# Two transformer layers in one program: an opening in another order, the step between the layers by token tile, expert flags read ahead

## The reference, cut to what matters

```python
def reference(x, c, ..., c_2, ctx_2, ...):
    x = first_block(x, c, ...)
    return second_block(x, c_2, ctx_2, ...)

def first_block(...):
    mod = (silu(c) @ w_ada + b_ada)[:, None, :]
    sh1, sc1, ga1, sh2, sc2, ga2 = split(mod, 6, axis=-1)
    h = rmsnorm(x, ln1_pre) * (1.0 + sc1) + sh1
    proj = h @ w_in                       # attention, HGRN2 and gates
    ...
    x = x + ga1 * rmsnorm(mix, ln1_post)
    h = rmsnorm(x, ln2_pre) * (1.0 + sc2) + sh2
    y = hierarchical_moe(h, ...)          # 32 experts, 2 of them per token
    x = x + ga2 * rmsnorm(y, ln2_post)

def second_block(...):                    # hybrid_layer, then rms_norm(x, final_norm_g)
    h = rms_norm(x, norm_mix_g) * (1 + sc_mix) + sh_mix
    p_in = h @ w_in + b_in
    hc = rms_norm(ctx, norm_mix_g) * (1 + mod_ctx[d:]) + mod_ctx[:d]
    ...
    x = x + g_mix * (merged @ w_out)
    h2 = rms_norm(x, norm_ffn_g) * (1 + sc_ffn) + sh_ffn
    y = moe_ffn(h2, ...)                  # a shared expert, and 64 experts, 8 of them per token
    x = x + g_ffn * y
```

## Time and profile before

| | us |
|---|---|
| median of 3 runs | 2428.25 (2425.47 to 2430.88) |
| the profiled execution | 2415.87 |
| its span | 2414.1 |
| PE busy / DVE / ACT / POOL | 2010.9 / 923.0 / 552.9 / 401.2 |
| granted TensorE clock, mean | 0.933 of full speed |

### The profile page before, as it was taken

How to read it: one execution, slowest core, us unless ns; L and a number is a source line. 1 busy time by engine, 2 the same in 40 slices (tenths; PEclk the granted TensorE clock), 3 DMA queues, 4 the chain that set the end, 5 groups by cost and what they waited for, 6 DMA issues and landing times.

```text
span 2414.1 us, 33274 instructions
## 1 busy us (share of the span) xinstructions
PE 2010.9 (83%) x13566; PEld 1361.5 (56%) x13567; DVE 923.0 (38%) x2043; ACT 552.9 (23%) x1018; POOL 401.2 (17%) x379
## 2 busy tenths in 40 slices
PE   3899989688781698996776998987999998999875
PEld 2677778454341686784444665754555555555432
DVE  2144552532214225215766122224443444434325
ACT  2132412211112214114665110020111111111111
POOL 0000000222211000001100000001444545444320
PEclk8899999699996797899999999978999999999998
DMA  6654530689993212012110122214899999999967
GB/s 258 243 227 175 210 123 12 237 338 417 417 386 134 79 53 70 18 53 79 48 48 2 61 88 104 97 53 169 350 360 357 400 404 402 365 358 395 382 247 311
DMA packets 97403, 514.79 MB, mean 213 GB/s; under 512 B 25154, under 2 KB 26210, under 8 KB 43100
## 3 DMA queue, kind: packets, MB, share of 16 engines
q1 hardware_dynamic: 62592, 449.60, 47.2%
q0 software_dynamic: 29504, 51.31, 6.0%
q10 hardware_dynamic: 5148, 11.59, 1.4%
HBM read 508.87 MB, written 49.81 MB: 231 GB/s over the span
## 4 chain that ended last, share of the span: by engine, by line
PE 68%; DVE 10%; DMA 10%; ACT 7%; issue 3%; ACTq 1%; POOL 0%; SPq 0%; DVEq 0%; POOLq 0%
PE ps L249 29%; PE ps L1689 16%; PE ps L1756 8%; DMA arena<-in_egu 7%; PE ps L1655 2%; ACT arena L2773 2%; DVE arena L2809 2%; PE ps L402 2%; DMA arena<-in_ada 2%; PE ps L1743 1%; ACT arena L2784 1%; PE ps L2758 1%; DMA arena<-y_rows 1%; PE ps L424 1%; ACT arena L267 1%
## 5 line engine op out<-in xcount | busy, mean ns | idle before, releaser
L1689 PE MATMUL ps<-arena 128*64 128x256 f32 x4096 | 479.4, 388 | 54.0 <-DMA arena<-in_egu 35.9
L1689 PEld LDWEIGHTS ps<-arena 128*64 128x64 f32 x4096 | 301.4, 140 | 256.3 <-DMA arena<-in_egu 66.2
L249 PE MATMUL ps<-arena 128*128 128x256 f32 (+4 forms) x1276 | 323.4, 416 | 2.4 <-DVE arena L491 1.3
L249 PEld LDWEIGHTS ps<-arena 128*128 128x128 f32 (+1 forms) x1276 | 229.0, 203 | 92.7 <-issue 71.2
L1756 PE MATMUL ps<-arena 128*64 128x512 f32 x1024 | 243.4, 604 | 37.0 <-issue 29.1
L1637 POOL DMA_INDIRECT arena<-h_rows,arena x160 | 193.2, 1208 | 312.6 <-DVE arena L1618 162.6
L1643 POOL DMA_INDIRECT y_rows<-arena x160 | 160.2, 1002 | 419.2 <-DVE arena L1787 369.6
L1751 DVE COPY arena<-ps 128x256 f32<-128x256 f32 (+1 forms) x96 | 36.5, 380 | 431.9 <-PE ps L1743 431.9
L1730 ACT ACTIVATE arena<-ps 128x256 f32<-128x256 f32 (+1 forms) x96 | 33.4, 348 | 503.8 <-PE ps L1689 503.8
L300 DVE TENSOR_TENSOR wlb<-arena,whb 128x1024 fp32r<-128x1024 f32 (+1 forms) x46 | 55.7, 1213 | 242.1 <-ACT whb L292 242.1
L1756 PEld LDWEIGHTS ps<-arena 128*64 128x64 f32 x1024 | 67.7, 136 | 134.7 <-issue 131.0
(11 more groups left out here) (392 smaller groups left out, 3062.2 us busy)
## 6 DMA issues: line engine op xcount, KB each, us to landing
arena<-in_egu SPq DMA_DIRECT2D x204, 1024.0 KB, 12.4
arena<-in_ed SPq DMA_DIRECT2D x102, 1024.0 KB, 8.4
arena<-in_ada SPq DMA_DIRECT2D x48, 1024.0 KB, 7.1
arena<-in_win SPq DMA_DIRECT2D x33, 1024.0 KB, 4.9
arena<-y_rows SPq DMA_DIRECT2D x20, 1024.0 KB, 13.9
arena<-in_wout SPq DMA_DIRECT2D x8, 1024.0 KB, 6.8
arena<-in_nabias POOLq DMA_DIRECT2D x16, 512.0 KB, 3.9
h_rows<-arena ACTq DMA_DIRECT2D x8, 512.0 KB, 2.9
```

The costliest lines, as they stand in the source:

```text
L249: z = pe.matmul(o, l, r, start=start and i == 0, stop=stop and i == len(pairs) - 1, skip_group_check=check)
L1689: z = pe.matmul(b[64 * j:64 * j + 64, 256 * s:256 * s + 256], XV[:, c, 64 * h:64 * h + 64], wk(k)[:, j * 256:j * 256 + 256], start=k == 0, ...
```

## The change

**Opening.** The 13 constants, and the attention bias table and two norm rows, are issued by POOL at its start; ACT issues only three loads. `x` comes in four transfers. The squares and the norm of `x` run on ACT before it copies the first `ada` sums. `PAIRS[1]` and `PAIRS[2]` change places, so that shift and scale of features 0 to 511 come first; the modulation runs over features 0 to 3 (of eight groups of 128) and then, behind `ada` pieces 2 and 3, over 4 to 7, its scaling by turns on ACT (even) and DVE (odd). The first weights are split in between. The first `win1` product waits for the first half only.

```diff
+        def act_start(act, w):
+            act_first(act, w)
+            act_cact(act, w)
+            act_floor(act, w)
+            act_norm(act, w, n1, x3, scr3, 4, lambda t: ld.to("x", t))
+            for n in range(2):
+                act_ada(act, w, n)
+            act_norm_split(act, w, n1, G1, MOD1[:, 0:8], HP1, range(4))
+            act_ada(act, w, 2)
+            for q in range(2):
+                act_hi(act, w, w1, 0, q, W1S, 2048, [n1.to("n", "T", 7)])
+            act_ada(act, w, 3)
+            act_norm_split(act, w, n1, G1, MOD1[:, 0:8], HP1, range(4, 8))
...
+        def pe_start(pe, w):
+            first, turns = [6, 7], [0, 1, 2, 3, 4, 5]
+            for n in range(2):
+                pe_ada(pe, w, n, first)
...
+            for n in (2, 3):
+                pe_ada(pe, w, n, first)
```

```diff
+            for t in range(4):
+                w.wait_ge(*ca.to("sum", t))
+                act.activation(scr3[:, t, :], sum1(t), ACT.Square, accum_out=small[:, t:t + 1]).then_inc(*ca.up("act", "sq", t))
+                act_root(act, w, ca, ("a", t), small[:, 8 + t:9 + t])
+                if t:
+                    act_tile_cols(act, w, nx, t - 1, G2, S2, xt_cols)
+                    act_hi_part(act, w, t - 1, 0)
...
+            act_hi(act, w, w2, 0, 0, W2S, width2(0), [ca.to("x", 1)])
...
         def pe_v(pe, w):
-            w.wait_ge(*nx.to("hlo", 7))
-            w.wait_ge(*nc_.to("h", 7))
-            w.wait_ge(*l2.to(*L2))
             for i in range(4):
-                pe_w2_tokm(pe, w, i, 256, BIN[0:1, i * 256:(i + 1) * 256])
+                pe_w2_tokm(pe, w, i, 256, BIN[0:1, i * 256:(i + 1) * 256], (lambda t: nx.to("hlo", t)) if i == 0 else None)
+                if i == 1:
+                    for k in range(8):
+                        w.wait_ge(*nc_.to("xn", 1))
+                        pe_turn(pe, w, nc_, "n", k, lambda t: CXN[:, t, k * 128:(k + 1) * 128], ("h", k), 2)
```

```diff
+            for t in range(4):
+                pe_rows_tile(pe, w, v2, MT, t)
+                if t:
+                    pe_tile_turn(pe, w, n3, t - 1, acc3)
+                if t >= 2:
+                    pe_tile_router(pe, w, n3, wr2, 64, t - 2, ("sc",))
+            pe_tile_turn(pe, w, n3, 3, acc3)
+            for t in (2, 3):
+                pe_tile_router(pe, w, n3, wr2, 64, t, ("sc",))
+            for t in range(4):
+                pe_tile_major(pe, w, n3, t)
```

```diff
+        def pe_flag(pe, w, x, e):
+            if x.V == 2 and e < x.E:
+                w.wait_ge(*x.st.to("big"))
+                flags[e] = pe.value_load(x.big[0:1, e:e + 1], min_val=0, max_val=1)
...
-                with pe.If(pe.value_load(x.big[0:1, e:e + 1], min_val=0, max_val=1) > 0):
+                with pe.If(flags.pop(e) > 0):
```

More of the change, by code:

```diff
@@ new lines, in dve_start @@
+        def dve_start(dve, w):
+            dve_cact(dve, w)
+            dve_floor(dve, w)
+            dve_norm_rows(dve, w, n1, x3, scr3, 4)
+            for half in range(2):
+                for n in (2 * half, 2 * half + 1):
+                    dve_ada(dve, w, n)
+                w.wait_ge(*ada.to("mod", 2 * half + 1))
+                h = slice(4 * half, 4 * half + 4)
+                dve.scalar_tensor_tensor(G1[:, h], MOD1[:, 8 + 4 * half:12 + 4 * half], 1.0, ln1p[:, h], ALU.add, ALU.mult).then_inc(
+                    *n1.up("dve", "G", half))
+                w.wait_ge(*n1.to("G", half))
+                dve_norm_split(dve, w, n1, G1, MOD1[:, 0:8], HP1, range(4 * half, 4 * half + 4))
+                if half == 0:
+                    dve_consts(dve, w)
+                    for q in range(2):
+                        dve_lo(dve, w, w1, 0, q, W1S, 2048)
@@ L678, in act_win1 @@
         def act_win1(act, w):
-            w.wait_ge(*n1.to("hlo", 7))
-            for q in range(2):
-                act_hi(act, w, w1, 0, q, W1S, 2048)
             for p in range(NJ1):
@@ L2212, in sp_xa @@
             sp_further(sp, w, xa, fa)
-            ring.order[:] = [i for i in ring.order if i < NS]
-            sp_results(sp, w, xa, fa, ca, 0, 4)
+            w.wait_ge(*fa.st.to("over"))
+            for t in range(4):
+                s = ring.turn(ca, ("rows", t), ("x", t), [RES1[t]])
+                for f in s.free:
+                    w.wait_ge(*f)
+                sp.dma_start(s.ap, Y1.rearrange("(p k h) d -> p (k h d)", k=2, h=2)[t * 128:(t + 1) * 128, :]).then_inc(*s.up())
         def pe_xa(pe, w):
@@ L2297, in pe_l2 @@
-            pe_norm(pe, w, nc_, scr3, 2, "h")
+            TB1[:] = [4, 5]
+            for t in range(4):
+                pe_tile_turn(pe, w, nx, t, scr3)
         def dve_l2(dve, w):
@@ L3091, in pe_program @@
             w = Waits(pe)
-            for n in range(4):
-                pe_ada(pe, w, n)
-            pe_norm(pe, w, n1, scr3, 4, "full")
+            pe_start(pe, w)
             pe_win1(pe, w)
@@ L3171, in sp_program @@
             sp_first(sp, w)
-            for n in range(4):
-                sp_ada(sp, w, n)
+            sp_start(sp, w)
             sp_win1(sp, w)
```

356 lines of the change are left out of this document (208 added, 148 removed).

## The result

The changed kernel takes 2347.26 us (median of 4 runs, 2343.45 to 2350.65) where the kernel before takes 2426.86 (2416.51 to 2430.88): a ratio of 0.9678, interval 0.9642 to 0.9713. The prediction was 2346. The profiled execution of after took 2349.86 us, with a span of 2348.0.

The account below looks back on a forecast made before the run. PE was taken as the engine most of the span hangs on, with DMA nearly full in layer 2's experts. 22.2 - 2.3 + 20 + 17 + 25 = 81.9 us off 2415.87 gives 2334.0, plus 12.4 makes 2346; range 2322 to 2388.

Parts of the forecast that it names:

- the 12.4: Whole kernel: us by which the median before stood above its profiled execution, added to 2334.0 to forecast 2346.
- Opening, 22.2 forecast: Opening: PE would start `win1` at 41.2 instead of 63.40, a gain of 22.2 us; bounds 13 to 25.
- six transposes by 28: Opening: six transposes done by 28 us, with norm and first half of the modulation lying under the transfers.
- POOL's constants come late: Rival, opening: constants land at 46, PE starts at 50, gain only 13, total 2355; chance 0.12.
- Layer 1's experts, -2.3 forecast: Layer 1's first gate: the numbering block ahead of the spread makes it 2.3 us later; between 0 and 3.
- slots come free with PE's progress, so the stretch behind it starts later too: Layer 1's experts: the DMA-bound stretch behind the first gate also starts 2.3 us later.
- Layer 1's end, +20 forecast: Layer 1's end, tile by tile: `v` starts 26.2 us earlier, two costs come back, net gain 20; between 12 and 24.
- w_out to the experts, +17 forecast: From `w_out` to layer 2's first gate: gain 17 us, between 12 and 20.
- Flags, +25 forecast: Layer 2's experts: reading flags ahead removes down's 29 us of waits, less 4 for DMA, gain 25; bounds 0 and 29.
- I take 4 off: Layer 2's experts: 4 us taken from the flags' 29 because PE will wait for weights in DMA-full stretches.
- PE now never waits for weights there: Layer 2's experts: the argument against the DMA-cap rival, which three experts' slots allow.
- the first rival: Layer 2's experts: DMA engines cap them, 12 of the flags' 29 us are left, total 2359; chance 0.2.

Follow-up runs that it names:

- after_again: The changed kernel once more, unedited, as base of the runs beside it: 2344.58 us, ratio 0.9686 to the kernel before.
- alibi_late: Changed kernel, but POOL issues alibi and the two norm rows (1.5 MB) only when piece 1 of `ada` is multiplied: 2352.45 us, ratio 0.97.
- fetch_bias: Changed kernel with the further pass's gathers one expert earlier and v's bias product waiting for bias rows and context alone: 2338.88 us, ratio 0.9655.
- wout_back: Changed kernel with `w_out`'s products and layer 2's norm, router, counts and numbering as in the kernel before: 2364.35 us, ratio 0.9765.
- flags_only: Kernel before, changed only in where the flag is read (a step ahead, one read for both uses): 2405.34 us, ratio 0.994.
- flags_back: Changed kernel with the flag read again at both branches: 2369.01 us, ratio 0.9792 to the kernel before.
- end1_back: Changed kernel with the end of layer 1 as before (all four tiles together, context and late loads behind them): 2361.55 us, ratio 0.9767.
- open_back: Changed kernel with the opening of the kernel before (constants on ACT's queue, modulation in one pass): 2366.47 us, ratio 0.9768.
- fetch_early: Changed kernel with the two gathers of the first further pass issued by POOL one expert earlier, both layers: 2345.24 us, ratio 0.969.
- half_ahead: Changed kernel, flags ahead, with half the bytes per weight piece from layer 2's fifth expert on (results differ): 2316.15 us.
- half_back: Changed kernel with the same halved transfers in layer 2's experts and the flag read again at both branches (results differ): 2360.69 us.

## Why the prediction was right, step by step

**The forecast's case came.** 2347.26 was measured where 2346 stood, and none of the rivals' times was nearer. That it came within 1.3 us is in part luck. 81.9 us were forecast. The medians lie 79.6 apart, with an interval of 70 to 87, and 75 in the set of after_again; the profiled executions only 66.0, 13.6 less than the medians, since one lies 11.0 below its median and the other 2.6 above. Adding the 12.4 was sound. But measured by single parts in the traces (15.5 to 18 for the opening, 20, 15 to 19, 12 to 18, and 0) the sum is 63 to 75, so opening and flags were reckoned too high, and the timed runs are too coarse to see it. The bounds of the whole were also added wrongly: the terms' bounds as they stand give 34 to 98 us and not 49 to 96, which is 2330 to 2394; the result lies in both.

**Opening, 22.2 forecast, 16.7 at the place, about 16 by layer 1's gate.** The step that was too short is "six transposes by 28". The total of bytes was nearly right: the last landing was reckoned at 37, and DMA windows were full until about 39 (the DMA share is 0.80 from 36 to 40). But I let pieces 0 and 1 land in the order of issue, with PE at work from about 12; its first product waited until 16.24. They shared the engines with POOL's 2.7 MB and with what SP had issued behind them, so piece 1 came at 28.08, and folds (3.4) and transposes (6.0) went behind it on PE, not under the transfers. So the products of pieces 2 and 3 came as one block of 3.6 us behind the transposes, where I had 1 us for a last half piece. Another 1.35 us stands ahead of the first product: its releaser is L506, the modulation of the second half, though the product needs only the first. By the code the product's bank is the one that a transposed group of the second half lies in (group 4, which ACT's L521 reads at 45.81, at the same time as L506). That was read, not tried. The bounds of 13 to 25 held it. "POOL's constants come late" didn't come true: `dve_consts` ran from 39.9 to 41.1 without a wait.

The Trainium skill (Trainium Kernel Development and Optimization, Key Constraints) has it that queues of different engines share the 16 DMA engines. The runs agree, with alibi_late's rows as the number: 1.5 MB moved behind piece 1 let it land 2.8 us sooner and pieces behind it later.

**Layer 1's experts, -2.3 forecast, -1.55 at the gate, 0 in time.** The step "slots come free with PE's progress, so the stretch behind it starts later too" was wrong: the first wait for expert weights ends 82.1 us after the same row with the block ahead and 82.6 with it behind.

**Layer 1's end, +20 forecast, 20 measured.** Its parts were right as well: a tile step of 8.15 was 7.7 to 8.4, 37 us to the first `v` product were 35.2, transposes and late loads took 7 back. The late loads' wait was 2.9 for 3 forecast, and fetch_bias took it away.

**w_out to the experts, +17 forecast, 19.4 in the profiles, 15 to 18 undone.** The stretch was 126 to 129 for 128 forecast. Routers took 1.85 to 1.9 us a tile in place of 2.1. The sum has no term for the clock, though: some 11 us are idle time gone and 4 to 8 PE's higher clock (0.95 and 0.98 in the two profiles for 0.88). The old router's 3.1 us a tile, from which a part of the gain was reckoned, is of that kind: in wout_back it runs from 1560 to 1573, nearly all at the lower clock.

**Flags, +25 forecast, 12 to 18 in the traces, 14.5 and 25.7 by the timed runs.** That the read is the price was right: down's wait for issue is gone. What the traces show as mis-sized is the term "I take 4 off". Of 34.2 us of idle time that the flags take away with half the bytes, only 14 to 16.5 go with whole transfers. The gates' waits grow by 9 (11.1 to about 20) where with half the bytes they fall by 2, and the gather's by 4.6. The reason given against this, "PE now never waits for weights there", doesn't hold either: 11 us of waits stood ahead of the gates in the kernel before, put down to DVE and to issue, and with half the bytes 3.9 of them are left. That is the first rival, at more than the weight I gave it; by the traces its reckoning, "12 of the 29 are left", was as near as mine or nearer. A second part went to the clock, for which the sum has no term: in this stage 12 to 13 us of granted clock are lost in flags_only and the changed kernel, 8 in before and flags_back (last section). Also mis-sized was the read's cost without DMA: 34 us of idle time and not 29. Down's waits for issue alone are 32.6 there; the read ahead of a gate shows 1.0.

The Trainium skill (Advanced Engine Details and Errata, Control Flow Timing) gives 108 ns for a compare-and-branch. No run here times a branch alone; the row that bears on it is down's, where a branch now stands ahead with no wait for issue left.

## What to carry to other kernels

Undo each part by itself when a change has several: here the total was right to 1.3 us while the traces put two of its terms, 22 and 25, some 4 to 7 and 7 to 13 too high. Where PE and the DMA engines are both over 90% busy, price a stall on PE against the speed that transfers have left: half or more of what was gained on PE came back, most of it as longer waits ahead of the gates. Sum such waits over all their releasers, since the one that the profile names can be another engine that ended at about the same time. Look at PE's busy time and granted clock beside its idle time: in the `w_out` stage up to 8 of 19 us were the same instructions at a higher clock. When a transfer is moved to another queue, ask which pieces it now lands beside, not only when the last byte comes.

## What the runs showed of the hardware that was not expected

The granted clock differs between executions of the same instructions. Windows from the first `win1` product to layer 1's first gate, columns as in rows 1: end1_back, the changed kernel twice, fetch_bias, and last the old opening in open_back. The instructions are the same in the first four.

```profile
45.63:450.43 404.80, 355.06 (x2613) 292.54 (x2613) 170.89 (x400) 125.44 (x206) 12.12 (x9) 0.92 0.46 174
```

```profile
46.75:455.92 409.17, 358.89 (x2613) 295.09 (x2613) 170.98 (x400) 125.30 (x206) 12.13 (x9) 0.92 0.46 172
```

```profile
46.73:459.32 412.59, 362.38 (x2612) 298.44 (x2613) 170.98 (x400) 125.40 (x206) 12.14 (x9) 0.91 0.45 170
```

```profile
46.34:465.08 418.74, 368.48 (x2613) 302.94 (x2613) 170.92 (x400) 125.42 (x206) 12.15 (x9) 0.89 0.44 168
```

```profile
63.94:477.53 413.59, 363.17 (x2613) 299.71 (x2613) 168.38 (x396) 120.97 (x200) 12.08 (x9) 0.91 0.45 169
```

DVE's busy time agrees within 0.1 us in the first four, PE's goes from 355 to 368, and with it the length, from 404.8 to 418.7. The clock lost in a window is the sum, over the trace's records of the granted clock, of each stretch's length times the share that was not granted. It is 30.7, 34.1, 37.5, 44.4 and 38.9 us in these five. Length less lost clock is 374.1, 375.0, 375.0, 374.4 and 374.7, and 373.6 to 375.9 in all fourteen profiles of this study: here a microsecond of lost clock costs a microsecond of time. From the first `v` product to layer 2's first gate it is the same: the ten kernels that have both stages in the new form take 836.3 to 852.6 us, lose 37.1 to 53.6, and the rest is 798.4 to 802.2.

In the first profile of after the clock was low for a good part of 178 to 226 us, and with it the trace gave the impression that some 9.6 us of the opening's gain were lost there. From a row at 199.21 in before (178.05 in after) to one at 258.70 (247.12) it took 59.5 us in before and 69.1 in after. But between the same rows it took 65.8 in open_back and 66.0 in flags_only, which have the old opening, and 59.6 in flags_back and 59.5 in end1_back, which have the new one. So it comes and goes with either opening, and nothing is to be explained by the change; it also makes the first stretch of the profile before (469.18) 7 to 8 us shorter than in the two others with that opening.

In layer 2's experts 10 to 16 us are lost in nine of the ten kernels with flags ahead and whole transfers, 6.8 in the tenth (fetch_early), and 5 to 8 in the four without (before, flags_back, half_ahead, half_back). The gates wait 18 to 21 us in all ten, and 2 to 11.5 in the four, so all but fetch_early have long waits and a large loss together. Whether these waits bring the lower level about was not tried.
